# Multiplying the attention logits of two units of heads together, in every second step

## The chip, the cores and the metric

The kernel runs on one core of one Trainium2 chip. The metric is the time of one execution in microseconds (us); three runs of the kernel before gave 1822.33, 1822.5 and 1825.92, with a median of 1822.5.

The engines are named as the profile names them: PE is TensorE (the matrix multiplier; PEld are its weight loads), DVE is VectorE, ACT is ScalarE, POOL is GpSimd and SP is SyncE, which issues the loads from memory. PE writes its products to PSUM, a memory of eight banks of 128 partitions by 512 float32. DVE and ACT read ("drain") them from there.

## The reference

256 tokens of width 1024 pass through two small networks, one behind the other. What matters here are their three attentions, each with 8 heads of 64 channels. The first network has one over a compressed key and value (`mla`), where an index score picks the 64 best keys of each row. The second network has a forgetting attention (`fox`) and a windowed one with sinks (`swa`). The logits of one head are the product of its queries and keys over the 64 channels; cut to the core:

```python
# mla, with the latent products folded into k and v
logits = einsum('bthc,btkc->bthk', q_lat, c_sel) * (HEAD_DIM_A ** -0.5)
p = softmax(where(valid, logits, -inf))
# fox
s = einsum('bqhd,bkhd->bhqk', qb, k) * scale
s = s + cb[..., None] - c_k[:, :, None, :]
p = softmax(where(causal, s, -inf)); o = einsum('bhqk,bkhd->bqhd', p, v)
# swa
s = einsum('bnqhgd,bnkhd->bnhgqk', qb, kw) * (HEAD_DIM ** -0.5)
```

Around them stand the projections in and out, a state space mixer, two feed-forward networks, a short convolution and, at the end, a mixture of 64 experts whose weights (403 MB) are read from memory once.

## The kernel before

All work is written out by hand for each engine, in one order per engine; engines wait for each other through semaphores. Weights come through a ring of six slots of 2 MB; SP issues a load when the slot's last user is done. ACT rounds each slot to a high half (L1579, in the expert stage L1850) and DVE makes the low half (L1921, in the expert stage L2374), and PE multiplies with both.

**Units.** An attention is cut into six units (`UNITS`): for the first 128 tokens unit 0 holds the even heads 0, 2, 4, 6 and unit 1 the odd heads 1, 3, 5, 7, each with 128 keys; for the second 128 tokens units 2 and 4 hold two even heads each, units 3 and 5 two odd heads each, with 256 keys. So every unit fills one PSUM bank. Even heads lie in partitions 0 to 63 of the operands and odd heads in partitions 64 to 127; the multiplications contract over 64 rows.

**Steps.** `attention` on PE (L939 to L987) walks over the units in steps t: the logits of unit t (`logits`, L948; for `fox` first the sums of the forget gates, `forget_sums`, L926 to L930), then some other work that is handed in as `others[t]`, then the transposes of the probabilities of unit t-2 (`turn`, L957), then the product with the values of unit t-3 (`mix`, L971). `others` are for `mla` the four z projections (L895), the transposes of xs (L1131), the products cbT and the sums acs (L1138 to L1151) and the cumulative sums (L1158). For `fox` and `swa`, which run as one row of twelve units, they are the projections gs0 and gs1 in steps 0 and 1 and the four halves of gs2 and gs3 in steps 7 to 10 (all L852), then the branch projections pf (L1341).

**The way of one unit.** PE writes the logits; DVE masks them (L1994 for the fox sums, L2003 for the logits), takes the row maximum (L2006) and its negative (L2009); ACT takes the exponentials (L1600); DVE inverts the row sums (L2022); POOL scales the probabilities (L2571); PE turns them (L957); ACT copies them (L1586); PE multiplies them with the values (L971); DVE drains that (L2031, L2032). DVE's own order in step t is: mask unit t, invert unit t-1, drain the values' product of unit t-3, then its other work (`others`, such as scaling gs0 at L2294). A split of a weight slot (L1921) stands in step 3 of `mla` and in steps 1 and 9 of the row of twelve.

**Banks.** `PsumOrder` hands out the eight banks in turn, in the order in which the plan (`plan_attention`) adds tiles. A tile's bank is free when the tile that had it before was drained, and `begin` makes PE wait for that:

```python
def take(self, name):
    while self.cursor % 8 in self.claimed.values():
        self.cursor += 1
    bank = self.cursor % 8
    self.cursor += 1
    self.place[name] = (bank, self.last_user.get(bank))
    self.last_user[bank] = name
```

`emptied_as` gives tiles the drain counts that belong to them where an engine drains in another order than that of the plan.

Of the kernel before, what the change touches and what calls it, by code (L numbers as in the profile page):

```python
# [29 lines left out]
P = 128  # L30
# [10 lines left out]
DH = 64  # L41
# [34 lines left out]
UNITS = [(0, 0, (0, 2, 4, 6), P), (0, 4, (1, 3, 5, 7), P),  # L76
         (1, 8, (0, 2), T), (1, 10, (1, 3), T), (1, 12, (4, 6), T), (1, 14, (5, 7), T)]
# [177 lines left out]
def program(nc, d, out):  # L255
    with ExitStack() as ctx:
# [206 lines left out]
        O = PsumOrder(tile_ready, act_drained, dve_drained)  # L463
# [4 lines left out]
        def plan_norm(n):  # L468
            for j in range(4):
                O.add(f"norm{n}_{j}", "dve" if n in SPLIT_NORMS or j % 2 else "act")  # L470

        def plan_attention(kinds, others):

            items = [(kind, u) for kind in kinds for u in range(len(UNITS))]
            for t in range(len(items) + 3):
                if t < len(items):
                    kind, u = items[t]
                    if kind == "fox":
                        O.add(f"fox_b{u}", "dve")
                    O.add(f"{kind}_l{u}", "dve")  # L480
                for other in (others[t] if t < len(others) else ()):
                    O.add(*other)
                if 2 <= t < len(items) + 2:
                    kind, u = items[t - 2]
                    O.add(f"{kind}_t{u}", "act")
                if t >= 3:
                    kind, u = items[t - 3]
                    O.add(f"{kind}_o{u}", "dve")

        Z_TILES = [f"z{tc}{h}" for h in range(2) for tc in range(NT)]  # L490

# [157 lines left out]
        def bank(name):  # L649
            return psum[:, O.bank(name), :]  # L650
# [146 lines left out]
        def _(pe):  # L797
            mm = nc.tensor.matmul
            seen = [0]

            def begin(name):

                if O.bank_free(name):
                    pe.wait_ge(*O.bank_free(name))

            def end(name, ins):
                seen[0] += 1
                assert O.ready(name)[1] == seen[0], name
                ins.then_inc(tile_ready, 1)
# [128 lines left out]

            def attention(kinds, others):  # L939

                def logits(kind, u):
                    q, k_of, _ = OPERANDS[kind]
                    tc, _, heads, w = UNITS[u]
                    name = f"{kind}_l{u}"
                    begin(name)
                    for i, h in enumerate(heads):
                        a = DH * (h % 2)
                        last = mm(bank(name)[:, i * w:(i + 1) * w], q[a:a + DH, h // 2, tc * P:(tc + 1) * P],  # L948
                                  k_of(h)[a:a + DH, 0:w], start=True, stop=True)
                    end(name, last)  # L950

                def turn(kind, u):
                    name = f"{kind}_t{u}"
                    pe.wait_ge(probs_ready, KINDS[kind] * NU + u + 1)
                    begin(name)
                    for blk in range(4):
                        last = nc.tensor.transpose(bank(name)[:, blk * P:(blk + 1) * P],  # L957
                                                   pr[:, u % 2, blk * P:(blk + 1) * P], ident)
                    end(name, last)

                def mix(kind, u):
                    v_of = OPERANDS[kind][2]
                    tc, _, heads, w = UNITS[u]
                    name = f"{kind}_o{u}"
                    pe.wait_ge(*O.drained(f"{kind}_t{u}"))
                    begin(name)
                    ns = w // P
                    for i, h in enumerate(heads):
                        a = DH * (h % 2)
                        for s in range(ns):  # L970
                            last = mm(bank(name)[a:a + DH, i * P:(i + 1) * P], v_of(h, s),  # L971
                                      pT[:, u % 2, (i * ns + s) * P:(i * ns + s + 1) * P],
                                      start=(s == 0), stop=(s == ns - 1))
                    end(name, last)

                items = [(kind, u) for kind in kinds for u in range(NU)]
                for t in range(len(items) + 3):
                    if t < len(items):
                        if items[t][0] == "fox":
                            forget_sums(items[t][1])  # L980
                        logits(*items[t])
                    if t < len(others):
                        others[t]()
                    if 2 <= t < len(items) + 2:
                        turn(*items[t - 2])
                    if t >= 3:
                        mix(*items[t - 3])  # L987
# [69 lines left out]
            for _ in range(5):  # L1057
                mm(bank("ik").rearrange("p (a b) -> p a b", a=4), ident, ident.unsqueeze(1).to_broadcast([P, 4, P]),
                   start=True, stop=True)
# [3 lines left out]
            for k in range(KD):  # L1063
# [5 lines left out]
                for tc in range(NT):  # L1069
                    for i, (a, w) in enumerate(hi_lo_passes(xnT_r, xn_r, high_half("misc"), ring_r[W.slot("misc")])):  # L1070
                        last = mm(bank(f"misc{tc}")[:, 0:280], a[:, k, tc * P:(tc + 1) * P], w[:, k * N_MISC:k * N_MISC + 280],
                                  start=(k == 0 and i == 0), stop=(k == KD - 1 and i == 2))
# [9 lines left out]
            for u, (tc, _, heads, wd) in enumerate(UNITS):  # L1082
                name = f"il{u}"
                begin(name)
                for i, h in enumerate(heads):
                    a = DH * (h % 2)
# [1666 lines left out]
```

## Time and profile before

| | |
|---|---|
| median of three runs | 1822.5 us (1822.33 to 1825.92) |
| span of the profiled execution | 1824.2 us |
| PE / PEld / DVE / ACT / POOL busy | 95% / 81% / 86% / 67% / 7% of the span |
| read from memory | 542.33 MB, mean 298 GB/s |
| chain that ended last | PE 59%, DMA 14%, issue 7%, DVE 6%, ACT 5% |
| `mla` attention | from 95.08 us; its last L971 ends near 143.8 us |
| `fox` and `swa` attentions | from 752.20 us; their last L971 ends near 828.9 us |
| expert stage | from about 873 us to the end |

The profiled execution has no separate time beside its span; the span stands 1.7 us over the median and within the spread of the three runs. Busy shares are averages over stages with different bounds. In the profile a float32 product of `logits` leaves two MATMUL records, so a unit of four heads shows as x8 and one of two heads as x4.

### The profile page before, as it was taken

Reading aid. Unit: us, or ns where it says so; the run is one execution under the profiler, and the core shown is the slowest. Engines: PE = TensorE matmul, PEld = TensorE weight load, DVE = VectorE, ACT = ScalarE, POOL = GpSimd, SP = SyncE. Lnnn points to the kernel's source line nnn. Section 1 sums busy time; section 2 is a strip of 40 time slices with the busy share of each in tenths; the row PEclk is TensorE's granted clock in tenths of the full one; section 3 lists DMA queues with packets and bytes.
Section 4 is the critical chain, followed back from the end, with each engine's and each line's share of the span. In section 5 each row is a group of like instructions: output and inputs, shape, how many; then the busy total and the mean of one; then the engine's idle time right before and its main releaser. Section 6 shows DMA issues by size and latency. Waiting matters only on the chain.

```text
span 1824.2 us, 25140 instructions
## 1 busy us (share of the span) xinstructions
PE 1739.8 (95%) x9700; PEld 1482.6 (81%) x9700; DVE 1577.6 (86%) x1372; ACT 1219.3 (67%) x949; POOL 127.5 (7%) x140
## 2 busy tenths in 40 slices
PE   8999999999999999999999999989999999999997
PEld 7977888889888889988877877778777787787775
DVE  5787777789577776677999999999999999999997
ACT  5465454443333345445788988889898898888985
POOL 1255000000000000441000000000000000000000
PEclk9999999999999999999999999999999999999999
DMA  7521345553345545326799999999999999999994
GB/s 286 192 93 70 139 176 203 211 233 145 127 185 184 195 197 203 121 88 251 303 427 427 428 429 428 428 429 429 428 429 429 428 429 428 428 429 428 429 428 193
DMA packets 40644, 544.11 MB, mean 298 GB/s; under 512 B 4624, under 2 KB 4752, under 8 KB 5904
## 3 DMA queue, kind: packets, MB, share of 16 engines
q1 hardware_dynamic: 40592, 543.39, 72.4%
q8 instruction: 36, 0.59, 0.1%
q14 instruction: 16, 0.13, 0.0%
HBM read 542.33 MB, written 1.05 MB: 298 GB/s over the span
## 4 chain that ended last, share of the span: by engine, by line
PE 59%; DMA 14%; issue 7%; DVE 6%; ACT 5%; POOL 0%; DVEq 0%; ACTq 0%; POOLq 0%; SPq 0%
PE psum L1439 16%; DMA ring<-in_w 14%; PE psum L1003 9%; PE psum L852 7%; PE psum L1020 6%; PE psum L1005 4%; PE psum L1453 4%; ACT arena_r L1850 4%; DVE ring_r L2374 3%; PE psum L1468 2%; PE psum L895 2%; PE psum L1203 1%; PE psum L912 1%; PE psum L1377 1%; PE psum L1341 1%
## 5 line engine op out<-in xcount | busy, mean ns | idle before, releaser
L2374 DVE TENSOR_TENSOR ring_r<-ring,arena_r 128x4096 fp32r<-128x4096 f32 x192 | 846.6, 4418 | 16.7 <-ACT arena_r L1850 13.0
L1850 ACT ACTIVATE arena_r<-ring 128x4096 fp32r<-128x4096 f32 x188 | 682.4, 3630 | 61.7 <-DMA ring<-in_w 61.1
L1439 PE MATMUL psum<-arena_r,stream_r 128*128 128x512 f32 x1024 | 409.5, 400 | 11.8 <-DVE stream_r L2464 9.2
L1439 PE MATMUL psum<-ring_r,stream_r 128*128 128x512 f32 x1024 | 401.9, 392 | 0.0
L1003 PE MATMUL psum<-stream_r,arena_r 128*128 128x512 f32 x704 | 250.4, 398 | 1.7 <-DVE stream_r L1936 1.7
L1439 PEld LDWEIGHTS psum<-arena_r,stream_r 128*128 128x128 f32 x1024 | 194.0, 189 | 57.0 <-DVE ring_r L2374 11.3
L1637 ACT ACTIVATE arena_r<-ring 128x3072 fp32r<-128x3072 f32 x40 | 111.0, 2775 | 181.1 <-DMA ring<-in_ffn 181.1
L1439 PEld LDWEIGHTS psum<-ring_r,stream_r 128*128 128x128 f32 x1024 | 194.0, 189 | 38.7
L1005 PE MATMUL psum<-stream_r,ring_r 128*128 128x256 f32 x704 | 197.5, 280 | 0.0
L1468 PE MATMUL psum<-arena_r 128*128 128x512 f32 x512 | 161.2, 396 | 11.7 <-DVE arena_r L2523 10.8
L852 PE MATMUL psum<-stream_r,ring_r 128*128 128x256 f32 x968 | 167.2, 284 | 0.0
L1003 PEld LDWEIGHTS psum<-stream_r,arena_r 128*128 128x128 f32 x704 | 132.3, 188 | 34.2 <-issue 2.1
L1468 PE MATMUL psum<-ring_r,arena_r 128*128 128x512 f32 x512 | 158.3, 390 | 0.0
L852 PEld LDWEIGHTS psum<-stream_r,ring_r 128*128 128x128 f32 x968 | 138.2, 192 | 2.2 <-issue 1.8
L1005 PEld LDWEIGHTS psum<-stream_r,ring_r 128*128 128x128 f32 x704 | 132.9, 189 | 1.6
L2079 DVE TENSOR_TENSOR ring_r<-ring,arena_r 128x3072 fp32r<-128x3072 f32 x40 | 134.0, 3351 | 0.0
L1468 PEld LDWEIGHTS psum<-arena_r 128*128 128x128 f32 x512 | 93.7, 188 | 36.5 <-DVE arena_r L2523 14.1
L2555 POOL TENSOR_SCALAR stat<-stat 128x1 f32<-128x1 f32 x22 | 9.8, 446 | 1520.2 <-ACT xn L1894 949.1
L1468 PEld LDWEIGHTS psum<-ring_r,arena_r 128*128 128x128 f32 x512 | 96.1, 188 | 20.8
L1020 PE MATMUL psum<-arena_r 128*128 128x512 f32 x352 | 103.3, 395 | 2.7 <-DVE arena_r L2072 2.7
L1453 PEld LDWEIGHTS psum<-small,arena 128*128 128x128 f32 x512 | 63.6, 191 | 47.5 <-ACT arena L1866 33.2
L1453 PE MATMUL psum<-small,arena 128*128 128x64 f32 x512 | 67.7, 275 | 30.0 <-ACT arena L1866 30.0
(336 smaller groups left out, 2482.9 us busy)
## 6 DMA issues: line engine op xcount, KB each, us to landing
ring<-in_w SPq DMA_DIRECT2D x192, 2048.0 KB, 12.9
ring<-in_ffn SPq DMA_DIRECT2D x44, 1536.0 KB, 6.4
ring<-in_w_in SPq DMA_DIRECT2D x8, 2048.0 KB, 8.0
ring<-in_in_w SPq DMA_DIRECT2D x7, 2048.0 KB, 12.5
ring<-in_out_w SPq DMA_DIRECT2D x7, 2048.0 KB, 8.1
ring<-in_l_in SPq DMA_DIRECT2D x8, 1536.0 KB, 8.7
ring<-in_proj SPq DMA_DIRECT2D x2, 2048.0 KB, 8.0
ring<-in_misc SPq DMA_DIRECT2D x1, 1632.0 KB, 8.9
```

Source lines behind the costliest of these rows:

```text
L852: last = mm(dst, w[:, at:at + width], a[:, k, :], start=(k == 0 and i == 0), stop=(k == KD - 1 and i == 2))
L895: last = mm(bank(name)[:, 0:width], a[:, k, tc * P:(tc + 1) * P], w[:, k * n:k * n + width], start=(k == 0 and i == 0), stop=(k == KD - 1 ...
L1003: mm(gu[b % 2][m], u_hi[:, at:at + P], both_halves[:, :, k, :], start=(k == 0), stop=(k == KD - 1), skip_group_check=True)
L1005: return mm(gu[b % 2][m][:, 1, :], u_lo[:, at:at + P], xnT_r[:, k, :], start=False, stop=(k == KD - 1), skip_group_check=True)
L1020: last = mm(bank(f"ffn{n}_{tc}{h}"), a[:, b % 2, tc * P:(tc + 1) * P], w[:, 2048 + h * 512:2560 + h * 512], start=(start and i == 0), stop ...
L1439: last = mm(dst, xg[:, k, :], b[:, k * D_EXPERT:(k + 1) * D_EXPERT], start=(k == 0 and b is u_hi), stop=(k == KD - 1 and b is u_lo))
L1453: last = mm(psum[:, T_BANK, (i * NE + j) * CAP:(i * NE + j + 1) * CAP], h_raw[:, e % 2, i, j * P:(j + 1) * P], turn, start=True, stop=True)
L1468: last = mm(psum[:, Y_BANK[h], :], hT[:, e % 3, j, :], b[:, j * D + h * 512:j * D + (h + 1) * 512], start=(e == 0 and j == 0 and b is u_hi ...
L1637: A(arena_r[:, FFN_HIGH[n][nxt % FFN_RING]:][:, 0:FFN_WORDS], ring[:, slot, 0:FFN_WORDS], ACT.Copy).then_inc(w_high, 1)
L1850: A(w_hi[u % HI_SLOTS], ring[:, MOE_SLOT[at], :], ACT.Copy).then_inc(m_hi, 1)
L2079: V.tensor_tensor(ring_r[slot][:, 0:FFN_WORDS], ring[:, slot, 0:FFN_WORDS], arena_r[:, FFN_HIGH[n][nxt % FFN_RING]:][:, 0:FFN_WORDS].bitca ...
L2374: V.tensor_tensor(ring_r[MOE_SLOT[u % NM]][:, :], raw, w_hi[u % HI_SLOTS].bitcast(F32), ALU.subtract).then_inc(m_lo, 1)
```

## The change

The logits of units 0 and 1, 2 and 3, 4 and 5 are multiplied in the even steps, both units of a pair in one call: head by head in turn, one of the even unit, one of the odd unit. For `fox` the forget sums of both units come ahead of that. Nothing is multiplied that wasn't before, and the steps of `turn`, `mix` and `others` stay. The plan of the banks follows: at even steps it adds the tiles of both units, at odd steps none. The order of DVE, ACT, POOL and SP is the same as before, row by row; only PE's order, the bank of a tile and the counts that are waited for change.

```diff
+        def logit_tiles(pair):
+            return ([f"fox_b{u}" for kind, u in pair if kind == "fox"] + [f"{kind}_l{u}" for kind, u in pair])
+
         def plan_attention(kinds, others):
             items = [(kind, u) for kind in kinds for u in range(len(UNITS))]
+            emptied = []
             for t in range(len(items) + 3):
-                if t < len(items):
-                    kind, u = items[t]
-                    if kind == "fox":
-                        O.add(f"fox_b{u}", "dve")
-                    O.add(f"{kind}_l{u}", "dve")
+                if t % 2 == 0:
+                    for name in logit_tiles(items[t:t + 2]):
+                        O.add(name, "dve")
+                emptied += logit_tiles(items[t:t + 1])
...
+            O.emptied_as(*emptied)
...
-                def logits(kind, u):
...
+                def logits(pair):
+                    for kind, u in pair:
+                        begin(f"{kind}_l{u}")
+                    for i in range(4):
+                        for kind, u in pair:
+                            q, k_of, _ = OPERANDS[kind]
+                            tc, _, heads, w = UNITS[u]
+                            if i < len(heads):
+                                h = heads[i]
+                                a = DH * (h % 2)
+                                last = mm(bank(f"{kind}_l{u}")[:, i * w:(i + 1) * w],
+                                          q[a:a + DH, h // 2, tc * P:(tc + 1) * P], k_of(h)[a:a + DH, 0:w],
+                                          start=True, stop=True)
+                                if i == len(heads) - 1:
+                                    end(f"{kind}_l{u}", last)
...
-                    if t < len(items):
-                        if items[t][0] == "fox":
-                            forget_sums(items[t][1])
-                        logits(*items[t])
+                    if t < len(items) and t % 2 == 0:
+                        for kind, u in items[t:t + 2]:
+                            if kind == "fox":
+                                forget_sums(u)
+                        logits(items[t:t + 2])
```

**PE in `mla`, steps 4 and 5, before.** L948 are logits, L1131 the transposes of xs (the first row of four tiles is shown), L957 and L971 transposes and values' product of an earlier unit, L1138 is B_tok and L1144 is cbT. Brackets name the semaphores that are waited for.

```order
L948 MATMUL psum<-arena 128x256 [waits act_drained]
L948 MATMUL psum<-arena 128x256
L1131 MATMUL psum<-small,arena 128x128 [waits dve_drained,conv_done]
...
L957 MATMUL psum<-small,arena 128x128 [waits act_drained,probs_ready]
L957 MATMUL psum<-small,arena 128x128 x3
L971 MATMUL psum<-arena 64x128 [waits act_drained]
L971 MATMUL psum<-arena 64x128 x3
L948 MATMUL psum<-arena 128x256 [waits dve_drained]
L948 MATMUL psum<-arena 128x256
L1138 MATMUL psum<-small,arena 128x128 [waits dve_drained]
L1138 MATMUL psum<-small,arena 128x128
L1144 MATMUL psum<-arena 128x128 [waits act_drained]
```

The same place now; lines have moved (L960 for L948, L1146 for L1131, L971 for L957, L985 for L971, L1153 and L1159 for L1138 and L1144).

```order
L960 MATMUL psum<-arena 128x256 [waits dve_drained,act_drained]
L960 MATMUL psum<-arena 128x256 x3
L1146 MATMUL psum<-small,arena 128x128 [waits dve_drained,conv_done]
...
L971 MATMUL psum<-small,arena 128x128 [waits act_drained,probs_ready]
L971 MATMUL psum<-small,arena 128x128 x3
L985 MATMUL psum<-arena 64x128 [waits dve_drained,act_drained]
L985 MATMUL psum<-arena 64x128 x3
L1153 MATMUL psum<-small,arena 128x128 [waits dve_drained]
L1153 MATMUL psum<-small,arena 128x128
L1159 MATMUL psum<-arena 128x128 [waits dve_drained]
```

The logits of unit 5 have left the place between L971 and L1138 and stand beside those of unit 4. cbT, whose bank was xs00's (drained by ACT), now takes the bank of the logits of unit 5, which DVE drains: its wait is on `dve_drained`.

**PE in `swa`, steps 9 and 10, before.** L852 is a half of gs3 (many rows, the first is shown), L948 the logits of units 3 and 4, L957 and L971 as above.

```order
L971 MATMUL psum<-arena 64x128 [waits act_drained]
L971 MATMUL psum<-arena 64x128 x3
L948 MATMUL psum<-arena 128x256 [waits dve_drained]
L948 MATMUL psum<-arena 128x256
L852 MATMUL psum<-stream_r,ring_r 128x256 [waits dve_drained,w_low]
...
L957 MATMUL psum<-small,arena 128x128 [waits dve_drained,probs_ready]
L957 MATMUL psum<-small,arena 128x128 x3
L971 MATMUL psum<-arena 64x128 [waits act_drained]
```

The same place now (L860 for L852).

```order
L985 MATMUL psum<-arena 64x128 [waits act_drained]
L985 MATMUL psum<-arena 64x128 x3
L860 MATMUL psum<-stream_r,ring_r 128x256 [waits dve_drained,w_low]
...
L971 MATMUL psum<-small,arena 128x128 [waits dve_drained,probs_ready]
L971 MATMUL psum<-small,arena 128x128 x3
L985 MATMUL psum<-arena 64x128 [waits act_drained]
```

No logits stand ahead of gs3 any more. Both before and now its bank had logits of `swa` in it; they were those of unit 2, and are now those of unit 3.

## Rows read from the trace of the kernel before

**Rows 1.** The page: engine shares, then busy tenths in 40 slices of the span.
```profile
PE 1739.8 (95%) x9700; PEld 1482.6 (81%) x9700; DVE 1577.6 (86%) x1372; ACT 1219.3 (67%) x949; POOL 127.5 (7%) x140
...
DMA  7521345553345545326799999999999999999994
```

**Rows 2.** Timeline of SP: start, length, the loads of expert weights.
```profile
830.61 34.98 SPq L756 DMA_DIRECT2D ring<-in_w  x6
...
883.28 74.01 SPq L756 DMA_DIRECT2D ring<-in_w  x17
```

**Rows 3.** Stretches: PE, PEld, DVE, ACT, POOL busy, PE's granted clock, DMA share, GB/s.
```profile
880.00:900.00 20.00, 20.00 (x100) 16.74 (x99) 19.14 (x11) 14.48 (x10) 0.00 (x0) 1.00 0.78 307
900.00:920.00 20.00, 19.93 (x104) 16.77 (x104) 20.00 (x9) 18.50 (x14) 0.00 (x0) 1.00 1.01 431
...
1000.00:1100.00 100.00, 96.69 (x503) 80.94 (x503) 99.41 (x44) 88.20 (x56) 0.00 (x0) 1.00 1.01 428
```

**Rows 4.** Timeline of PE, index logits, then what follows; start, length.
```profile
38.17 3.41 PE L1087 MATMUL psum<-arena 64*128 64x128 f32 x32 [0.83 <-issue]
...
41.51 1.10 PE L852 MATMUL psum<-stream_r,ring_r 128*128 128x256 f32 x7
```

**Rows 5.** Timeline of PE in `mla`; in brackets idle time and its releaser.
```profile
95.08 1.16 PE L948 MATMUL psum<-arena 64*128 64x128 f32 x8
96.17 5.74 PE L895 MATMUL psum<-ring_r,stream_r 128*128 128x512 f32 x24
...
116.55 0.65 PE L957 MATMUL psum<-small,arena 128*128 128x128 f32 x4 [1.18 <-POOL arena L2571]
117.14 1.13 PE L948 MATMUL psum<-arena 64*128 64x256 f32 x4
118.19 7.34 PE L895 MATMUL psum<-ring_r,stream_r 128*128 128x512 f32 x24
...
131.32 1.13 PE L948 MATMUL psum<-arena 64*128 64x256 f32 x4
...
132.66 1.06 PE L1144 MATMUL psum<-arena 128*128 128x128 f32 x8
```

**Rows 6.** Timeline of DVE in `mla`: draining unit 1, masking unit 5.
```profile
131.43 0.69 DVE L2031 CAST arena_r<-psum 64x512 fp32r<-64x512 f32 x1 [1.30 <-PE psum L971]
...
132.89 0.69 DVE L2003 SCALAR_TENSOR_TENSOR arena<-psum,arena 128x512 f32<-128x512 f32 x1
```

**Rows 7.** Stretch of the slow L895 (columns as in rows 3).
```profile
118.40:121.80 3.40, 3.40 (x9) 2.63 (x9) 3.09 (x13) 0.90 (x3) 0.41 (x1) 0.50 0.00 0
```

**Rows 8.** Timeline of PE in `fox` and `swa`.
```profile
752.20 1.16 PE L926 MATMUL psum<-small,stat 128*128 128x128 f32 x8 [0.73 <-ACT arena L1586]
...
760.22 1.05 PE L926 MATMUL psum<-small,stat 128*128 128x128 f32 x8
...
770.82 0.66 PE L957 MATMUL psum<-small,arena 128*128 128x128 f32 x4
...
775.00 0.66 PE L957 MATMUL psum<-small,arena 128*128 128x128 f32 x4 [1.13 <-POOL arena L2571]
...
800.00 1.13 PE L948 MATMUL psum<-arena 64*128 64x256 f32 x4
801.05 3.14 PE L852 MATMUL psum<-stream_r,ring_r 128*128 128x256 f32 x24
...
815.57 0.66 PE L957 MATMUL psum<-small,arena 128*128 128x128 f32 x4 [0.24 <-POOL arena L2571]
```

**Rows 9.** Timeline of DVE and POOL in `fox` and `swa`.
```profile
764.15 4.39 DVE L1921 TENSOR_TENSOR ring_r<-ring,ring_r 128x4096 fp32r<-128x4096 f32 x1
...
800.10 0.43 DVE L2031 CAST arena_r<-psum 64x256 fp32r<-64x256 f32 x1 [2.28 <-PE psum L971]
...
801.75 0.69 DVE L2003 SCALAR_TENSOR_TENSOR arena<-psum,small 128x512 f32<-128x512 f32 x1
...
764.41 6.35 POOL L2571 TENSOR_SCALAR arena<-arena,stat 128x128 f32<-128x128 f32 x4 [17.86 <-DVE stat L2022]
```

More of the change, by code:

```diff
@@ L470, in plan_norm @@
                 O.add(f"norm{n}_{j}", "dve" if n in SPLIT_NORMS or j % 2 else "act")
+        def logit_tiles(pair):
+            return ([f"fox_b{u}" for kind, u in pair if kind == "fox"] + [f"{kind}_l{u}" for kind, u in pair])
         def plan_attention(kinds, others):
             items = [(kind, u) for kind in kinds for u in range(len(UNITS))]
+            emptied = []
             for t in range(len(items) + 3):
-                if t < len(items):
-                    kind, u = items[t]
-                    if kind == "fox":
-                        O.add(f"fox_b{u}", "dve")
-                    O.add(f"{kind}_l{u}", "dve")
+                if t % 2 == 0:
+                    for name in logit_tiles(items[t:t + 2]):
+                        O.add(name, "dve")
+                emptied += logit_tiles(items[t:t + 1])
                 for other in (others[t] if t < len(others) else ()):
                     O.add(*other)
+                    if other[1] == "dve":
+                        emptied.append(other[0])
                 if 2 <= t < len(items) + 2:
@@ L488, in plan_attention @@
                     O.add(f"{kind}_o{u}", "dve")
+                    emptied.append(f"{kind}_o{u}")
+            O.emptied_as(*emptied)
         Z_TILES = [f"z{tc}{h}" for h in range(2) for tc in range(NT)]
@@ L939, in attention @@
             def attention(kinds, others):
-                def logits(kind, u):
[L942 to L950, printed above, removed]
+                def logits(pair):
[13 more added lines that the diff above has]
+                                    end(f"{kind}_l{u}", last)
                 def turn(kind, u):
```

## The prediction

> **What bounds the kernel now.** The page comes first: PE is busy 95% of the span, DVE 86%, and the DMA engines only fill up in the second half [rows 1]. The expert stage is bound by its loads: SP issues the first six loads as slots come free, the seventh at 883.28 us, when PE has finished with the first expert weight, and from 900 us on memory gives 427 to 431 GB/s [rows 2, 3]. So the end follows that seventh issue: what PE gains or loses ahead of it, it gains or loses in the end. Ahead of it the chain of waits runs over PE for most of its length, so the places to look at are the three attentions, where PE takes turns with DVE, ACT and POOL. There the timeline of PE shows the idle times and whom they are for [rows 5, 8], and the timelines of DVE and POOL what these do in that time [rows 6, 9].
>
> **What the pairing removes.** Six units of logits in `mla` stand alone between other products. A unit of four heads takes from 95.08 to 96.17, 1.09 us; one of two heads from 117.14 to 118.19, 1.05 us [rows 5]. The eighteen units of the three attentions are 6 x 1.09 + 12 x 1.05 = 19.1 us of PE. What a pair costs, the kernel shows in its index logits, which have the same six shapes and stand one unit behind the other: they start at 38.17, and the next product starts at 41.51 [rows 4]. That is 3.34 us where the same shapes in `mla` take 2 x 1.09 + 4 x 1.05 = 6.38. Products of even heads (rows 0 to 63 of the array) and of odd heads (rows 64 to 127) clearly run at the same time there. 3.34 / 3 is 1.11 us for a pair. Bounds for a pair that stands alone are 1.05 us (one unit's time) and 2.14 us (both, one after the other). I take 1.2 us, near the index rows, with a little more because each pair now begins and ends between other products. Nine pairs save 9 x (2.14 - 1.2) = 8.5 us of PE's time. That is the most there is to gain.
>
> **What happens to it in mla.** PE's first stop is the transpose of unit 0 at 116.55, after 1.18 us of waiting for POOL [rows 5]. POOL ends with unit 0 by DVE's time, and DVE only comes to mask unit 0 after its index and convolution work, which the change doesn't touch. So the 0.9 us of the first pair only lengthen that wait, to some 2.1 us. Unit 3's logits, which stood behind the wait, are now ahead of it: from here PE is 1.05 us earlier. It stays 0.9 us earlier through z11, the first values' product and the pair of units 4 and 5, until the product of unit 1, which ended at 131.32 and would end at 130.4. Unit 5's logits no longer follow (1.06 us), B_tok does, and then cbT. But cbT's bank is now that of unit 5's logits, and DVE masks unit 5 after it has drained the product of unit 1. That drain and the mask took from 131.32 to 132.89 + 0.69 = 133.58, 2.26 us [rows 6]. So cbT can start at 130.4 + 2.26 = 132.7. It started at 132.66 [rows 5]. The whole gain of this stage is given back there: term 0.0.
>
> The bound on the other side comes from the clock. The 24 products of z11 took 7.18 us (118.19 to 125.37) because the granted clock stood at 0.5, 1.2 GHz, from 118.4 to 121.8, behind the idle stretch and some small products [rows 5, 7]. At full clock such a group takes 5.7. If that slow stretch falls elsewhere, POOL's unit 2 is the next to hold PE, cbT starts about 1.0 us earlier, and the term is -1.0.
>
> **What happens to it in fox and swa.** I take the lists in their new order with the durations of the rows.
> - The start is the same, 752.20. Two units' sums (0.98 each) and the pair now stand ahead of gs0, 1.2 us more than one unit's sums and logits. DVE drains gs0 before it masks unit 1 and inverts unit 0, then it splits a weight slot for 4.39 us. POOL's scaling of unit 0, which took 6.35 us and ended with that split [rows 9], moves with all that: the first transpose moves from 770.82 to about 771.9. PE waits 0.8 us for it.
> - The second transpose was at 775.00, after unit 3's sums and logits had filled most of the wait [rows 8]. These are now ahead. DVE inverts unit 1 0.5 us later, so the transpose comes at 775.5, and PE is idle for it some 2.8 us.
> - Step 4 now has two units' sums (1.4 us each) ahead of unit 4's logits: they end at 781.1 in place of 779.2. DVE waits there, and what hangs on it (inverting unit 3, POOL, the transposes of units 3 and 4) comes 1.2 to 1.4 us late. The first pair of `swa` gives 0.9 of it back, and a half of gs2 starts 0.3 late.
> - The product of `fox` unit 5 ends at 800.5 in place of 800.0, and gs3 follows at once. But its bank is now that of `swa` unit 3. DVE drains the `fox` product, scales gs2, and only then masks unit 3: from 800.0 to 801.75 + 0.69, 2.44 us [rows 9]. gs3 starts at 803.0, where it started at 801.05 [rows 8]: 1.9 us late.
> - From there nothing gives it back. The product of `swa` unit 0, DVE's split behind it, masking unit 4, and the transpose that PE waited for at 815.57 [rows 8] follow each other. The saved 0.9 us of the last pair lies in front of that wait and is lost. Term: +2.0.
>
> DVE, ACT and POOL keep their orders. SP's loads wait for PE's tiles and move with it: the loads that follow gs0 to gs3 are up to 2 us late, with DMA far from full there. They carry no term.
>
> **The sum.** 0.0 + 2.0 = +2.0 us on the profiled span of 1824.2. Against the median of 1822.5, 1.7 below that span, it makes **1824.5 us**. The three runs lie within 3.6 us of each other, so 0.2% (3.6 us: below 1818.9 or above 1826.1) is about what a measurement can tell from no change.
>
> A rule of the Trainium skill points away from both the gain and the loss: TensorEngine Tiling (Array Packing), PSUM Bottleneck, says that tiling speeds up TensorE but not the emptying of PSUM. By it alone the pairing is worth nothing, and the time stays at 1822.5. This trace agrees that DVE's draining holds the attentions, and adds what the rule doesn't say: that the banks are taken earlier.
>
> **Rivals.**
> - *PE's time is the bound and the 8.5 us come through: 1814.0.* For it: PE is busy 95%, and the chain lies on PE. Against it: at 116.55, 775.00 and 815.57 PE waits for POOL in the very stages that change, and all pairs but a few lie in front of such a wait. It needs DVE to be ready earlier than I work out. 0.07.
> - *DVE holds both ends and the new waits cost less than I think: 1822.5, give or take 1.3.* gs3's wait or that of cbT would be shorter if DVE got to its masks earlier. This is also where the skill's rule would put it. 0.21.
> - *Slower, by the clock.* PE now has idle stretches of 2 us and more at about 114.5, 128, 772 to 775 and 800.5, where it had 1.2 at most. One such stretch before z11 was followed by 3.4 us at half clock and cost 7.18 - 5.7 = 1.5 us. This decides from the point where one or more of the new stretches does the same in work that nothing hides; one to three of them make 1826.0 to 1829.0. Against it: the idle stretch of 1.13 at 775.00 [rows 8] had no such sequel. The Trainium skill, in TensorE: Matmul & The Clock Gate, Part 1, says that the slow clock is the default and that activity releases it, which would make the stretches of idleness matter; the half clock of rows 7 agrees. 0.20.
> - *The pair doesn't overlap as the index logits do.* Then a pair costs 2.14 us, the odd unit's time lies ahead of everything in the even steps, and about six of nine pairs are on the path, 6 x 0.94 = 5.6 us more: 1830.1. Against it: rows 4. 0.06.
>
> **How the numbers follow.** My forecast, 1823.3 to 1826.1, has 0.46. Faster than 1818.9 is only the first rival: 0.07. Slower than 1826.1 are the pair that doesn't overlap (0.06), most of the clock's rival (0.17) and a tail of the forecast (0.02): 0.25. Within 0.2% is the rest: 0.68. The range from 1820.5 to 1828.5 leaves out the first and the last rival and the far end of the third, less than 0.2 in all, and takes in -1.0 in `mla` and one or two slow stretches.
>
> **What would show it.** In the profile after: an L960 group of eight products that lasts about 1.2 to 1.3 us; cbT (L1159) starting about 2 us behind B_tok (L1153), waiting for DVE's L2018 (the old L2003); gs3's first L860 about 2.5 us behind the last L985 before it; the first transpose of `fox` near 771.9 and idle time ahead of the second. The seventh expert load should be issued near 885.3 us, with the rest of the span as long as before. I am wrong if gs3 starts without a wait, if the expert loads come earlier than 883.3, or if an L960 group takes over 2 us.

## The result, and the profile after

The changed kernel takes **1831.05 us** (median of six runs, 1829.92 to 1832.05). The kernel before, run beside it, takes 1824.13 (1822.33 to 1826.10). The ratio is 1.0037, with a 95% interval of 1.0027 to 1.0047: slower by 4.9 to 8.6 us. The prediction was 1824.5, with a range up to 1828.5. It started from a median of 1822.5 for before; three more runs moved that to 1824.13, so 1.6 us of the miss lies in the starting point, and the rest is a difference of +6.9 where +2.0 was forecast.

The shares of busy time hardly move, and don't show the loss. The page of the profile, engine shares:

```profile
PE 1735.4 (95%) x9700; PEld 1481.9 (81%) x9700; DVE 1578.7 (86%) x1372; ACT 1219.5 (67%) x949; POOL 126.9 (7%) x140
```

The timeline of SP shows that the end is made ahead of the expert stage. The seventh expert load is issued at 889.28, where before it was at 883.28 [rows 2], 6.0 us later; the span grew by 5.9, from 1824.2 to 1830.1. Behind that issue nothing changed.

```profile
836.59 34.98 SPq L764 DMA_DIRECT2D ring<-in_w  x6
...
889.28 67.28 SPq L764 DMA_DIRECT2D ring<-in_w  x16
```

So the stages ahead of it are compared one by one. "mla" is the time from the first logits to the start of the last product with the values; "row of twelve" the time from the first fox sums to the start of the last `ps` product (the projection that follows the last product with the values), both from the start times of single records of the trace.

| profiled run | to mla | mla | between | row of twelve | to the end |
|---|---|---|---|---|---|
| before | 95.08 | 48.54 | 608.58 | 89.62 | 982.34 |
| changed | 96.22 | 50.49 | 606.97 | 94.12 | 982.27 |
| difference | +1.14 | +1.95 | -1.61 | +4.50 | -0.07 |

The first and the third difference lie where no instruction moved. Each goes with a half-clock stretch (1.2 GHz) that one run had and the other hadn't: 6.8 us long near 14 in the changed kernel where before had 3.4 us near 16, and 3.4 us near 668 in before alone. That is run-to-run noise (the later profiles, whose code is the same there, have 6.8, 3.4 or nothing near 14), and nearly cancels. What the change did is +1.95 in `mla` and +4.50 in the row of twelve.

**mla after** (timeline of PE; compare with [rows 5]; L960 is the pair of logits, L971 the transposes, L985 the product with the values):

```profile
96.23 1.16 PE L960 MATMUL psum<-arena 64*128 64x128 f32 x16
97.32 11.18 PE L903 MATMUL psum<-ring_r,stream_r 128*128 128x512 f32 x48
108.42 1.13 PE L960 MATMUL psum<-arena 64*128 64x256 f32 x8
...
117.70 0.66 PE L971 MATMUL psum<-small,arena 128*128 128x128 f32 x4 [2.48 <-POOL arena L2586]
118.12 5.71 PE L903 MATMUL psum<-ring_r,stream_r 128*128 128x512 f32 x24
...
129.01 0.66 PE L971 MATMUL psum<-small,arena 128*128 128x128 f32 x4 [0.77 <-POOL arena L2586]
129.60 1.09 PE L985 MATMUL psum<-arena 128*64 128x128 f32 x8
130.62 0.44 PE L1153 MATMUL psum<-small,arena 128*128 128x128 f32 x2
132.92 1.48 PE L1159 MATMUL psum<-arena 128*128 128x128 f32 x8 [1.87 <-DVE arena L2018]
...
136.36 1.97 PE L985 MATMUL psum<-arena 128*64 128x128 f32 x8
138.26 3.08 PE L1173 MATMUL psum<-small,stat 128*128 128x128 f32 x16
```

A pair costs 1.09 us from its start to the next product's, what one unit cost before. The next stop is the first transpose, with 2.48 us of idle time for POOL where there were 1.18. cbT waits 1.87 us for DVE's mask of unit 5, as worked out. Then comes what the sum didn't have: the product with the values at 136.36 takes 1.97 us and the sums at 138.26 take 3.08, where the same groups take 1.09 and 2.05 at full clock (shown below for e5).

**The row of twelve after** (timeline of PE; compare with [rows 8]; L934 to L938 are fox's sums, L860 projections):

```profile
772.98 0.66 PE L971 MATMUL psum<-small,arena 128*128 128x128 f32 x4 [0.71 <-POOL arena L2586]
776.56 1.12 PE L971 MATMUL psum<-small,arena 128*128 128x128 f32 x4 [2.92 <-POOL arena L2586]
777.61 1.97 PE L985 MATMUL psum<-arena 128*64 128x128 f32 x8
779.51 0.80 PE L934 MATMUL psum<-small,stat 128*128 128x128 f32 x2
...
788.52 0.74 PE L971 MATMUL psum<-small,arena 128*128 128x128 f32 x4 [2.16 <-POOL arena L2586]
789.19 1.97 PE L985 MATMUL psum<-arena 128*64 128x128 f32 x8
...
803.46 1.09 PE L985 MATMUL psum<-arena 128*64 128x128 f32 x8
807.07 3.10 PE L860 MATMUL psum<-stream_r,ring_r 128*128 128x256 f32 x24 [2.52 <-DVE arena L2018]
...
821.55 0.65 PE L971 MATMUL psum<-small,arena 128*128 128x128 f32 x4 [1.28 <-POOL arena L2586]
```

The waits of 0.71 and 2.92 us for POOL and gs3's 2.52 us for DVE are nearly to the tenth what the prediction said (0.8, 2.8, 2.4). Two products with the values take 1.97 us again. The stretches of the clock say why; columns are PE, PEld, DVE, ACT and POOL busy, PE's granted clock, DMA share, GB/s:

```profile
133.60:140.40 6.80, 6.80 (x33) 6.14 (x32) 2.17 (x7) 3.00 (x10) 1.82 (x2) 0.50 0.01 2
775.30:782.10 6.80, 5.54 (x24) 4.88 (x25) 2.55 (x6) 1.57 (x5) 3.03 (x5) 0.50 0.01 4
789.00:792.40 3.40, 3.40 (x22) 2.88 (x22) 2.39 (x6) 1.69 (x5) 1.68 (x2) 0.50 0.00 0
```

Three stretches at a granted clock of 0.5 stand in the changed stages, 17 us in all; before had one, of 3.4 us [rows 7]. By the Trainium skill, TensorE: Matmul & The Clock Gate, Part 1, the slow clock is the default and activity releases it. That would tie the stretches to the idle time ahead of them: 1.87, 2.92 and 2.16 us in the rows above. The experiments test it.

### The profile page after: what moved, and what is told of

The parts are those of the page before. It is cut to its first block, busy times and chain, and to the rows that moved or that the text cites. A ratio compares the mean times of both kernels' runs of the same rounds, so it can differ in the third digit from the quotient of the medians.

```text
span 1830.1 us, 25148 instructions
## 1 busy us (share of the span) xinstructions
PE 1735.4 (95%) x9700; PEld 1481.9 (81%) x9700; DVE 1578.7 (86%) x1372; ACT 1219.5 (67%) x949; POOL 126.9 (7%) x140
## 3 DMA queue, kind: packets, MB, share of 16 engines
HBM read 542.33 MB, written 1.05 MB: 297 GB/s over the span
## 4 chain that ended last, share of the span: by engine, by line
PE 60%; DMA 15%; issue 6%; ACT 5%; DVE 5%; POOL 0%; DVEq 0%; ACTq 0%; POOLq 0%; SPq 0%
PE psum L1454 18%; DMA ring<-in_w 14%; PE psum L1018 8%; PE psum L860 7%; PE psum L1035 6%; PE psum L1020 4%; PE psum L1468 4%; ACT arena_r L1865 3%; PE psum L1483 2%; PE psum L903 2%; DVE ring_r L2389 1%; PE psum L1218 1%; PE psum L920 1%; PE psum L1392 1%; PE psum L1356 1%
## 5 line engine op out<-in xcount | busy, mean ns | idle before, releaser
L860 PE MATMUL psum<-stream_r,ring_r 128*128 128x256 f32 x968 | 167.0, 284 | 2.5 <-DVE arena L2018 2.5
L860 PEld LDWEIGHTS psum<-stream_r,ring_r 128*128 128x128 f32 x968 | 138.2, 192 | 4.6 <-issue 4.4
```

Of the source, the lines that this page charges most:

```text
L860: last = mm(dst, w[:, at:at + width], a[:, k, :], start=(k == 0 and i == 0), stop=(k == KD - 1 and i == 2))
```

## The experiments

Theory 1: the loss is made of new waits (banks taken earlier, fox's sums of the odd unit ahead of everything in the even step) and of half-clock stretches that follow the longer ones. Against it stand that the waits alone are the loss, that the rest is noise, and that a pair has a hidden cost. All medians, and the stages as above with their half-clock stretches (start and length in us):

| run | median us | ratio to before, 95% | mla | half clock | row of twelve | half clock |
|---|---|---|---|---|---|---|
| before (profiled) | | | 48.54 | 118.4, 3.4 | 89.62 | none |
| changed | 1831.05 | 1.0037 (1.0027-1.0047) | 50.49 | 133.6, 6.8 | 94.12 | 775.3, 6.8; 789.0, 3.4 |
| e1 pairs in mla only | 1826.06 | 1.0011 (1.0002-1.0020) | 50.47 | 132.4, 6.8 | 89.62 | none |
| e2 pairs in fox and swa only | 1827.53 | 1.0020 (1.0010-1.0030) | 46.96 | none | 93.15 | 774.6, 3.4; 784.8, 3.4 |
| e3 unit by unit | 1833.11 | 1.0045 (1.0032-1.0059) | 50.50 | 134.0, 6.8 | 95.04 | 775.7, 6.8; 789.3, 3.4 |
| e4 filled | 1828.09 | 1.0021 (1.0012-1.0031) | 48.71 | none | 91.89 | none |
| e5 banks | 1826.28 | 1.0012 (1.0002-1.0022) | 46.77 | none | 91.78 | 771.0, 6.8; 784.6, 3.4 |
| e6 banks, filled | 1822.44 | 0.9991 (0.9981-1.0001) | 46.72 | none | 88.80 | none |
| e7 before, filled | 1823.19 | 0.9992 (0.9983-1.0001) | 46.99 | none | 89.62 | none |
| e8 banks, late sums | 1819.69 | 0.9977 (0.9968-0.9986) | 46.72 | none | 86.67 | none |
| e9 late sums only | 1826.82 | 1.0016 (1.0007-1.0025) | 50.48 | 131.7, 6.8 | 90.72 | 800.7, 3.4 |
| e10 e8, filled | 1819.98 | 0.9977 (0.9967-0.9988) | 46.71 | none | 86.65 | none |
| e11 before with the waits | 1827.89 | 1.0027 (1.0016-1.0038) | 49.67 | 117.8, 3.4 | 91.13 | none |
| e12 cbT filled | 1828.99 | 1.0028 (1.0019-1.0037) | 48.04 | none | 93.94 | 770.8, 6.8; 784.5, 3.4 |

The kernel before, timed beside them, had medians of 1824.56 (e1 to e4), 1824.28 (e5 to e8), 1823.63 (e9, e10) and 1823.85 (e11, e12); its single runs lie anywhere from 1821.3 to 1827.4.

**e1 and e2: one part of the change at a time.** Pairs are formed only for the kinds named (in e2 they are `fox` and `swa`); the others go unit by unit, as before. The plan asks the same function.

```diff
+        PAIRED = ("mla",)
+        def together(items, t):
+            if t >= len(items):
+                return []
+            if items[t][0] in PAIRED:
+                return items[t:t + 2] if t % 2 == 0 else []
+            return items[t:t + 1]
...
-                        logits(items[t:t + 2])
+                        logits(together(items, t))
```

> Only mla's logits are paired; fox and swa are as before. Theory 1 (new waits, and half-clock stretches behind them): cbT waits for DVE about 1.9 us and the saved time of the pairs is gone; with the half-clock stretch near 133 us instead of 118 us the stage from its first logits to L1218 takes 50.5 us where before it took 48.7: time +1 to +2 us. Theory 2 (waits alone, the clock has no part): 0, since the saved 1 us is given back at cbT. Theory 3 (the rest of the loss is no property of the change but of runs): +-0 with no half clock near 133.

> Only the row of twelve units is paired; mla is as before. Theory 1: +4 to +5 us (waits +2, half-clock stretches of 6.8 us behind the wait for POOL near 775 and of 3.4 us near 789 some 1.3 to 2.5 more); gs3's first L860 waits about 2.5 us for DVE. Theory 2: +2. The sum of this run's and e1's difference should be the whole +6.9.

Each attention reproduces its own part: 50.47 in `mla` with the half clock behind cbT, 93.15 in the row of twelve, while the other stage stays at before's length. The medians are 1.5 and 3.0 over before's; the sum, 4.5, is less than the 6.9 of the whole, and e2 alone is below the 4 to 5 us that were expected. e2's two stretches were 3.4 us each, not 6.8 and 3.4, which accounts for 1.0 of it (93.15 for 94.12). The other 1.4 us are no more than the intervals of the three ratios leave open, and have no cause shown.

**e3: is it the order head by head that makes a pair cheap?** Both units of a pair in the even step, one after the other.

```diff
-                    for i in range(4):
-                        for kind, u in pair:
...
+                    for kind, u in pair:
...
+                        for i, h in enumerate(heads):
```

> Both units of a pair in the even step as in the changed kernel, but one unit's heads after the other's. If the order head by head in turn is what makes them overlap, a group of eight products takes 2.1 us in place of 1.09, and the time is 4 to 5 us over the changed kernel where nothing hides it, near 1835; less if the longer groups shorten the idle stretches and the clock stays up. If the array overlaps the row halves also when a whole unit stands behind the other (as the index logits did), the group takes 1.1 to 1.3 us and the time stays at 1831.

The answer depends on the shape. Timeline of PE, the pair of four heads each and the first pair of two heads each:

```profile
96.40 1.71 PE L958 MATMUL psum<-arena 64*128 64x128 f32 x16
98.04 11.18 PE L903 MATMUL psum<-ring_r,stream_r 128*128 128x512 f32 x48
109.15 1.14 PE L958 MATMUL psum<-arena 64*128 64x256 f32 x8
110.22 5.73 PE L903 MATMUL psum<-ring_r,stream_r 128*128 128x512 f32 x24
```

With two heads per unit the pair takes 1.07 us in either order: nothing is lost by writing one unit behind the other. With four heads it takes 1.64 against 1.09, because the second unit starts 0.55 us behind the first, and only then do the two overlap. The whole kernel is 2.1 us over the changed one (1833.11 against 1831.05), not 4 to 5. So a pair hides no cost, and the loss isn't in the products.

**e4: PE kept busy in the waits.** Ahead of a wait, small products go to a bank that is free and overwritten later.

```diff
+            def keep_busy(name, n):
+                begin(name)
+                for _ in range(n):
+                    mm(bank(name)[:, 0:P], ident, tri, start=True, stop=True)
...
+                    if (kind, u) in {("mla", 0): 13, ("fox", 1): 16, ("fox", 3): 11}:
+                        keep_busy(name, {("mla", 0): 13, ("fox", 1): 16, ("fox", 3): 11}[kind, u])
...
+                keep_busy("acs", 9)
                 begin("cbT")
...
+                if name == "gs3" and m == 0:
+                    keep_busy("swa_t1", 12)
```

> The changed kernel with small products of ident and tri in the places where PE waits: 13 and 16 and 11 ahead of the first mla transpose and of fox's transposes 1 and 3, 9 ahead of cbT, 12 ahead of gs3. They go to a bank that is free and is overwritten later. Theory 1: with PE not idle the half-clock stretches at 133.6, 775.3 and 789.0 are gone or shorter, and the time falls by 2.5 to 4.5 us to 1826.5 to 1828.5. Theory 2: the waits' ends are set by DVE and POOL, so nothing changes: 1831 or up to 1 more.

All three half clocks are gone, and the median falls by 3.0, as Theory 1 said. Timeline of PE, second fox transpose:

```profile
770.12 3.74 PE L813 MATMUL psum<-small 128*128 128x128 f32 x32
773.70 0.60 PE L979 MATMUL psum<-small,arena 128*128 128x128 f32 x4
774.23 1.09 PE L993 MATMUL psum<-arena 128*64 128x128 f32 x8
```

PE does more work and starts this transpose 0.5 us later than in the changed kernel (23.4 against 22.9 us behind the first fox sums), and still what follows is faster: the product with the values takes 1.09 us for 1.97. The fillers were too long, by 0.3 to 0.5 us at the first transpose of `mla` and here, and by 1.0 at cbT (37.7 against 36.7 us behind the first logits), so the stages are overstated.

**e12: only cbT filled**, with 6 products in the bank of acs.

> The changed kernel with 6 small products ahead of cbT alone, in the bank of acs, for the 1.87 us in which PE waits there. Theory 1: no half clock behind cbT, mla takes 47.8 to 48.2 in place of 50.5, all else as in the changed kernel: the median falls by 2.3 to 2.7 to 1828.5. Rival (the half clock at 133.6 hangs on something else, such as the small sums behind cbT): it stays, and so does 1831.

Timeline of PE, the fillers and cbT:

```profile
130.42 1.60 PE L813 MATMUL psum<-small 128*128 128x128 f32 x12 [0.83 <-ACT xnT L1608]
131.86 1.06 PE L1166 MATMUL psum<-arena 128*128 128x128 f32 x8
```

`mla` takes 48.04 (expected 47.8 to 48.2), the half clock behind cbT is gone, and the row of twelve keeps its own two. The median fell by 2.1 (expected 2.3 to 2.7). Here cbT starts 15.61 us behind the first transpose, against 15.21 in e1 (131.71 - 116.50), so about 0.4 of the 48.04 is filler: the wait alone gives 47.64. That is 0.7 over the 46.96 and 46.99 that `mla` takes unit by unit when no half clock falls into it (e2, e7), and the half clock behind it costs 50.47 - 47.64 = 2.8.

**e5 and e6: other banks.** Two lines in the plan let cbT have xs00's bank again, and gs3 that of `fox_o4`; e6 has fillers too, fitted a little better (11, 13, 9), and none at cbT or gs3.

```diff
+                if kinds != ["mla"] and t == 10:
+                    O.claim("gs3", "swa_l4", "swa_l5")
...
+                if kinds == ["mla"] and t == 5:
+                    O.claim("B_tok", "mla_t3", "cbT", "acs")
```

> The changed kernel with two bank assignments altered: cbT takes the bank of xs00 again (mla_t3 takes that of mla's unit 5), and gs3 that of fox's last-but-one product instead of that of swa's unit 3. Theory 1 (the bank waits are a part of the loss): cbT no longer waits 1.87 us and gs3 no longer 2.52 us for DVE. In mla the time from the first logits to the last L985 falls from 50.5 to 48.0 or less, because the idle stretch ahead of the half clock at 133.6 is gone too; in the row of twelve the time from the first sums to the last ps product falls from 94.1 by 1 to 2.5. Total 1827.5 to 1829. Rival (the banks only name the wait, DVE's masks are what is late): the idle time moves to the next transpose or values' product and the total stays above 1830.

> As e5, and small products of ident and tri ahead of the first mla transpose (11) and fox's transposes 1 (13) and 3 (9), so that no half clock follows them. Theory 1: the row of twelve takes 90 to 91 us (before: 89.6), mla 46.5 to 47.5 (before: 48.5, of which a half-clock stretch made 1.6): total within 1 us of before's median, 1823.5 to 1826. If clock and banks are not the whole loss it stays above 1827.

e5, timeline of PE: cbT, the product and the sums that were slow in the changed kernel, and gs3 behind its product.

```profile
131.22 1.16 PE L1163 MATMUL psum<-arena 128*128 128x128 f32 x8 [0.83 <-ACT xnT L1605]
...
133.37 1.09 PE L989 MATMUL psum<-arena 128*64 128x128 f32 x8
134.38 2.05 PE L1177 MATMUL psum<-small,stat 128*128 128x128 f32 x16
...
798.98 1.09 PE L989 MATMUL psum<-arena 128*64 128x128 f32 x8
800.00 3.14 PE L864 MATMUL psum<-stream_r,ring_r 128*128 128x256 f32 x24
```

Both bank waits were real: gs3 now follows at once, cbT waits 0.83 instead of 1.87, and no half clock follows it. `mla` falls from 50.49 to 46.77, the row of twelve by 2.34. My total for e5 (1827.5 to 1829) was 1 to 3 us too high: `mla` fell by 3.7, where I had counted 2.5. e6 takes off the other two stretches, 2.98 us, and is 1.8 under before's median, with an interval of the ratio that still holds 1. I had expected 90 to 91 us for its row of twelve and 1823.5 to 1826 for the whole; both came out lower (88.80 and 1822.44).

**e11: the waits without the pairing.** The kernel before, unit by unit, with cbT made to wait for the drain of `mla_l5` and gs3 for that of `swa_l3`.

```diff
                 begin("cbT")
+                pe.wait_ge(*O.drained("mla_l5"))
...
+                    if name == "gs3":
+                        pe.wait_ge(*O.drained("swa_l3"))
```

> The kernel before, unit by unit, with the two waits alone: cbT waits until DVE has drained mla's unit 5, gs3 until it has drained swa's unit 3. Theory 1: cbT starts some 15.3 us behind the first mla transpose (e2: 14.5), gs3 1.4 to 2.5 us later than in before; without a half clock mla takes 47.5 to 48 (e2, e7: 47.0) and the row of twelve 91 to 92 (89.6); each half clock that follows adds 1.5 to 2.5. Total 1826.5 to 1829. If the waits need the pairing to hurt, it stays at 1824.3.

Timeline of PE, cbT and the first half of gs3:

```profile
133.13 1.13 PE L1145 MATMUL psum<-arena 128*128 128x128 f32 x8 [0.91 <-DVE arena L2006]
...
801.30 3.11 PE L852 MATMUL psum<-stream_r,ring_r 128*128 128x256 f32 x24 [1.47 <-DVE arena L2006]
```

The two waits alone cost 1.1 us in `mla` (49.67 against 48.54, each with a half clock in z11) and 1.5 in the row of twelve. They are shorter than in the changed kernel (0.91 and 1.47), and in the profiled run no half clock follows. The median is 4.0 over before, as expected (1826.5 to 1829) but more than the 2.6 of the two stages, with single runs up to 1834.1; what the slower ones had isn't seen, since they have no trace.

**e8: fox's sums back in their own step.** As e5, and only logits are paired: the odd unit's forget sums are multiplied in the odd step again, and the plan adds their tiles there.

```diff
-                    for name in logit_tiles(items[t:t + 2]):
+                    for name in logit_tiles(items[t:t + 1]) + [f"{kind}_l{u}" for kind, u in items[t + 1:t + 2]]:
                         O.add(name, "dve")
+                elif t < len(items) and items[t][0] == "fox":
+                    O.add(f"fox_b{items[t][1]}", "dve")
...
+                    if t < len(items) and items[t][0] == "fox":
+                        forget_sums(items[t][1])
                     if t < len(items) and t % 2 == 0:
-                        for kind, u in items[t:t + 2]:
-                            if kind == "fox":
-                                forget_sums(u)
                         logits(items[t:t + 2])
```

> As e5, and the forget sums of an odd unit stay in the odd step; only the logits of a pair are multiplied together. Since a pair costs what one unit did (1.09), step 0 and step 4 of fox are then as short as before. Theory 1 (the odd unit's sums, 1.0 and 1.4 us, are what makes fox's first steps late): gs0 starts 2.1 us behind the first sums (changed kernel: 3.1), the wait of 2.92 us for transpose 1 shrinks to about 1.9 or less, no half clock follows, and the row of twelve takes 88.5 to 90.5 us: total 1822.5 to 1826. If the lateness is DVE's own, the transposes stay where e5 has them.

Timeline of PE, fox's sums, its first two transposes, and the product behind the second; then the seventh expert load:

```profile
750.05 1.16 PE L940 MATMUL psum<-small,stat 128*128 128x128 f32 x8 [0.73 <-ACT arena L1606]
751.13 1.16 PE L966 MATMUL psum<-arena 64*128 64x128 f32 x16
752.23 6.01 PE L866 MATMUL psum<-stream_r,ring_r 128*128 128x256 f32 x48
...
768.68 0.66 PE L977 MATMUL psum<-small,arena 128*128 128x128 f32 x4 [1.40 <-POOL arena L2591]
...
772.14 0.66 PE L977 MATMUL psum<-small,arena 128*128 128x128 f32 x4 [1.46 <-POOL arena L2591]
772.72 1.09 PE L991 MATMUL psum<-arena 128*64 128x128 f32 x8
```

```profile
878.23 79.86 SPq L770 DMA_DIRECT2D ring<-in_w  x18
```

The wait of 2.92 is one of 1.40 and one of 1.46 now, no half clock follows, and the row of twelve takes 86.67, which is 3.0 less than before; I had expected 88.5 at best, and 1822.5 for the whole. **This version beats both kernels: 1819.69 us**, ratio 0.9977 (0.9968 to 0.9986), 4.6 under before.

**e9: the late sums with the changed kernel's banks, and e10: e8 with fillers.**

> As e8 but with the changed kernel's banks: only the odd unit's forget sums go back to the odd step. From e5 and e8: the row of twelve takes 86.7 (e8) plus gs3's wait, which was 2.5 us in the changed kernel and 2.3 of it came through (94.1 to 91.8): 89 us, no half clock behind fox's transposes; mla as in the changed kernel with cbT's wait and the half clock behind it, 50.5. Sum against e8: 2.3 + 3.7 = +6.0, about 1825.7. If banks and sums don't add up, it lies below 1824 or above 1827.5.

> As e8, with small products ahead of the first mla transpose (11) and of fox's transposes 0 and 1 (5 each), where 2.48, 1.40 and 1.46 us of waiting are left. If these waits still bring a half clock in some runs, the median falls 0.5 to 1.5 us below e8's 1819.7 and the highest run with it. If waits of this length without cbT's behind them bring none, it stays at 1819.7 give or take 0.5.

In e9 `mla` is 50.48 as foreseen. The row of twelve takes 90.72, not 89, because gs3's wait was followed by a half clock this time (timeline of PE):

```profile
800.34 4.60 PE L862 MATMUL psum<-stream_r,ring_r 128*128 128x256 f32 x24 [2.53 <-DVE arena L2019]
```

4.60 against 3.13 us is 1.5, and 90.72 less that is 89.2: the parts add up, and the median was 1.1 over the forecast. e10 equals e8 (1819.98 and 1819.69), so nothing is left to win by filling these waits.

**e7: fillers in the kernel before**, 4 products ahead of the first mla transpose and 4 ahead of fox's transpose 1.

> The kernel before with 4 such small products ahead of the first mla transpose and 4 ahead of fox's transpose 1, where it waits 1.2 and 1.1 us. The half clock at 118.4 was there in one profile of before and missing in e2, with the same wait of 1.17 ahead of it. If these idle stretches make the half clock of before, its runs lose the upper cluster (1825.5 to 1827.4) and the median falls by 1 to 1.6 to 1823. If its half-clock stretches have another cause, the median stays at 1824.5 give or take 0.7.

The median fell by 1.1, and the highest of 11 runs was 1824.90 where before reached 1827.4. The interval (0.9983 to 1.0001) still holds 1, so it is likely, but not shown, that before's own half clock at 118.4 hangs on the wait of 1.18.

## Why the prediction was wrong

**The pair's price** (1.2, bounds 1.05 and 2.14): measured 1.09 and 1.07. Right, and rows of the index logits were the right place to read it. That PE's saving is lost at the next wait held too.

**The waits**: those that the prediction priced stood where it put them. Ahead of fox's first two transposes they were 0.71 and 2.92 us for 0.8 and 2.8; gs3 waited 2.52 us for 2.4; and from the end of the product ahead of it to cbT it was 2.30 us (130.62 to 132.92) for 2.26. One was missing: the 2.16 us ahead of fox's fourth transpose (788.52), which the lateness of step 4 brings and a half clock follows. One row was misread on the way, without effect on the sum: POOL's scaling of unit 0 ended at 770.76, 2.2 us behind DVE's split (768.54) and not with it [rows 9].

**The term of mla** (0.0, bound -1.0). With full clock behind cbT the stage would take 47.64 (e12 less its filler) against the 48.54 of the profiled before: -0.9, the bound. The measured term is +1.95. The step that failed is "The whole gain of this stage is given back there: term 0.0", and with it the bound of -1.0: both put a half clock behind cbT at nothing. The prediction took the clock's stretch of before as fixed and asked only where it might fall, not what the new idle time at cbT would bring: 2.8 us of half clock.

**The term of fox and swa** (+2.0). In steps that runs show: with free banks and full clock the pairing gives 88.80 for 89.62, -0.8 (e6); gs3's bank adds 2.34 (changed less e5); the half clocks add 2.98 (e5 less e6). Together +4.5. Waits alone make +1.5, near the +2.0. The term was mis-sized by the clock: it put the half-clock stretches behind fox's second and fourth transpose at nothing, and they cost 2.98 us. Nearly as large is what the odd unit's early sums cost, 2.1 us (e6 less e8), which the prediction did count as lateness of the first steps and of step 4.

**The rival by the clock** (0.20, 1826.0 to 1829.0) was the right mechanism, with too small a chance and price. It took 1.5 us for a stretch, from a 3.4-us one in z11, and its range of the time ended at 1829.0, 2 us short of the 1831.05 measured. The stretches were 6.8, 6.8 and 3.4 us long, and cost 2.8 in `mla` and 3.0 in the row of twelve. The argument against it, that the idle stretch of 1.13 us at 775.00 had no sequel, compared 1.1 us with 2.9. e4, e6 and e12, which put products into such waits, lose the half clock. By the Trainium skill (TensorE: Matmul & The Clock Gate, Part 1) activity is what releases the slow clock; these three runs agree with it.

**The rival of PE's time** (0.07) was right in part: once banks and sums are out of the way, e8 gets 3.0 us through in the row of twelve, and 0.2 in `mla` (46.72 against 46.96). The other rivals fell: DVE doesn't hold both ends, and the pair overlaps.

**The end**: +6.0 at the seventh load and +5.9 in the span. The view that what PE loses ahead of that issue is lost at the end held in every profiled run: from the last `ps` product to the end it is 981.7 to 983.5, except in e4 and e6, with 986.5 and 987.0 (below). The prediction's signs of being wrong (gs3 without a wait, the loads earlier, a pair over 2 us) all stayed away: none of them looked at what follows a wait.

## What to carry to other kernels

Moving work on PE ahead of a wait doesn't only lengthen that wait. Ask what tile now takes whose PSUM bank, since banks handed out in turn change owners for every tile behind the move, and where PE gets a new idle stretch of some 2 to 3 us among small products, price a half-clock stretch behind it beside its own length (here 1.87, 2.16 and 2.92 us brought one each time; 1.9 to 2.5 us beside long products did in 1 of 12 cases). Pair only what costs nothing when paired (two row halves of the array), and leave at its place what doesn't overlap, such as fox's sums: that alone was worth 2.1 us (e6 to e8).

## What the runs showed of the hardware

- Which idle time brings a half clock: fox's second transpose, 2.92 us after sums, logits and transposes: 5 of 5 profiles without filler (changed, e2, e3, e5, e12). Fox's fourth transpose, 2.16 us some 12 us later: 5 of 5 (the same); where that wait is 0.62 us (e8, e9, e10): 0 of 3. cbT's 1.87 us, with 0.77 shortly ahead of it: 4 of 4 (changed, e1, e3, e9); with 0.83 in place of the 1.87 (e5, e6, e8, e10): 0 of 4. gs3's 2.52 us: 1 of 5 (e9). The first mla transpose, 1.9 to 2.5 us of waiting behind the long z products and with such products following: 0 of 7. With only 1.2 us there, but logits of two heads between it and the z product: 2 of 3 (before and e11, not e2). So the length of the idle time isn't all; what PE does around it counts. Which of the products matter stays open.
- Stretches of half clock also stand in the expert stage of every profile, behind shorter idle times. Before has 28 idle times of 0.9 to 1.7 us between 890 and 1810 us and half clock behind three of them (at 968.3, 1422.3 and 1555.4; the idle times are 0.97, 1.51 and 0.93 us, and small products for the router follow each). Memory gives 428 to 431 GB/s there [rows 3] and bounds that stage, and the times to the end in the table of stages show no cost.
- The half-clock stretches were 3.4, 6.8 or 10.2 us long, apart from the one that the end of the span cuts off. The last length was in the profiles of e4 (from 874.4) and e6 (from 870.5), at the start of the expert stage, where nothing was changed. The seventh expert load came 45.54 us behind the last `ps` product there, and 41.5 in the others: 4.1 us. Both have fillers in fox, but e7 and e10 have too and show none. What brings it wasn't tried; it is the likely cause of e6's upper runs (1826.1 to 1827.2, the profiled one among them, above a lower group of 1820.5 to 1822.9).
- Products of the two row halves overlap also when all of one unit stand ahead of the other's, fully with two heads (1.07 us) and in part with four (1.64).
